# First stage of a hybrid layer: decays and score ahead of the numerator's norm, and six smaller moves

## The chip, the cores and the metric

One Trainium2 chip, all eight cores, one program. Each core computes half the output rows of one of four sequences, with no traffic between cores. The metric is the device time in microseconds of the slowest core.

## The reference

```python
# one layer, x (4, 4096, 1024) f32
h = rmsnorm(x, norm_mix_pre)
q_m,k_m,v_m,i_m,f_m,o_m, q_f,k_f,v_f,f_f, g_a,g_b = split(h @ w_in)
# A: mLSTM, 4 heads, dqk 128, dv 256
log_i = 15*tanh((i_m+b)/15);  log_f = log_sigmoid(15*tanh((f_m+b)/15))
C_t = f_t C_{t-1} + i_t v_t k_t^T;  n_t = f_t n_{t-1} + i_t k_t
h_a = rmsnorm((C_t q_t) / max(|n_t.q_t|, 1), ml_head_norm) * sigmoid(o_m)
# B: forgetting attention, 8 heads of 128, F = cumsum(log_sigmoid(f_f + b))
h_b = softmax(q_t.k_s/sqrt(128) + F_t - F_s, s <= t) @ v_f
merged = sigmoid(g_a+ba) * (h_a @ w_branch_a) + sigmoid(g_b+bb) * (h_b @ w_branch_b)
x = x + rmsnorm(merged @ w_out, norm_mix_post)
# channel mixing: causal width-3 convolution between up-projection and gate
a, g = split(causal_dwconv(rmsnorm(x, norm_ffn_pre) @ w_up, conv_w, conv_b))
x = x + rmsnorm((gelu(g) * a) @ w_down, norm_ffn_post)
```

## The kernel before, in words

Each core has 32 blocks of 128 tokens. Blocks 0 to 14 are a prefix, of which only the mLSTM state and the attention's keys and values are needed; 15 to 31 are its own (15 for two edge tokens only). A small framework records operations per engine in program order and inserts semaphore waits from what each reads and writes. So **the order in which the Python code calls `pg.add` is the order of every engine's queue**, and each engine works its queue strictly in order. Stages follow each other: mixing stage (to about 445 us), attention, merge, output projection, channel mixing.

**Mixing stage.** `A_load`, `A_sq` (square on ACT, then `rms_rstd`: a DVE step and a power on POOL), `A_sc` (DVE) and `A_T` (eight transposes on TensorE, one DVE copy) bring a block in. `W_load` and `W_cast` bring the weights in, with casts on ACT, DVE or POOL. `A_G` multiplies a block by the 16 gate columns; after each eight blocks `gates_slot` turns them into log gates (DVE add, ACT tanh, DVE times 15, ACT exponential, ACT ln, DVE sign) and `gates_slot2`, a step later, into cumulative gates (two small f32 matmuls, ACT and DVE steps). Four such slots cover the 32 blocks.

The main loop runs over the blocks in the order `MSEQ` (0 to 14, 16 to 23, 15, 24 to 31), `c` the block now, `cn` the next. A prefix block costs K and V projections and `upd`, the state update (matmuls at L825 and L827, four DVE steps `stt` at L525). A block of the own part (sixteen with an output of 128 rows, and 15) goes through these steps, in queue order: `num_mm(c)` (numerator and normaliser on TensorE L776 to L787; squares on ACT L791; small DVE steps; power on POOL L803), `I_mm(cn)` (decay matmuls into bank `SB0`, score matmuls into `SB1`, exponential of the decays on ACT, mask on POOL L748), `k_trans(cn)`, `num_fin(c)` (norm and output gate: four DVE steps), `V_proj(cn, 0)`, `I_fin(cn)` (two DVE steps: scaled queries `qs`, and `ST` = score times masked decays, which frees `SB1`), `A_T` of an input block, `V_proj(cn, 1)`, `upd(c)` (whose first half writes `SB1`), `ctb` (state scaled on ACT, L533), `O_proj(cn)` (tanh on ACT; POOL adds one, L719). Every fourth block is *fresh*: `QK_proj` computes queries and keys of the next four blocks. mm groups all carry line 385, small DVE helpers lines 522 (`tt`), 525 (`stt`) and 529 (`sts`), ACT's helper line 533. At two blocks POOL also issues weight DMAs (`load_qk`, `load_v`, L349), and at eleven a conversion DMA (L849).

**Attention.** `proj_pieces(h)` gives projections of head h in pieces (q, k: L1067; v: L385), whose banks DVE empties (`evac`, L1044); head 0's run alone, the others' between the steps of the head before. A step is `qk(n+1)`, an exponential on ACT (L1188), `pv(n-2)` (L1208). Two edge queries per head go through `e_qk` (24 matmuls of two columns, L1124, a DVE step, exponential L1131) and `e_pv`.

**Merge and output.** The merge runs for each of eight column chunks over five token tiles (edge, then four of 512), each with four mm groups that read `haT`, `hbT` and `xnT_own`. The output projection takes two mm groups a block, then a square on ACT, `rms_rstd`, a DVE product (L1445), two additions and a second square; `E1_scale` (DVE, L1397) prepares blocks for the channel mixing.

## Time and profile before

| | |
|---|---|
| median of 3 runs | 1790.73 us (1788.42 to 1964.29) |
| profiled execution | 1789.04 us, span 1787.5 us on core 7 |
| spans of the cores | 1782.1 to 1787.5 us, mean granted clock 0.980 to 0.983 |
| TensorE (PE) busy | 1658.5 us (93%) |
| DVE / ACT / POOL busy | 843.6 (47%) / 905.0 (51%) / 520.1 us (29%) |
| chain that ended last | PE 81%, ACT 6%, DVE 5%, issue 5%, POOL 2% |

Times are microseconds from the start of the span. "Idle before" is the time that the engine stood still ahead of an instruction, with the one that released it. Matmuls are pipelined, so neighbouring ones overlap. Granted clock 1.00 is the 2.4 GHz level, 0.50 the 1.2 GHz level.

### The profile page before, as it was taken

To read this page: it belongs to the slowest core of one execution; us is meant where nothing else is said; L and a number is where in the kernel's file an instruction comes from. 1 tells how busy PE (TensorE), PEld (TensorE's weight loads), DVE (VectorE), ACT (ScalarE), POOL (GpSimd) and SP (SyncE) were. 2 spreads that over 40 slices of the span, in tenths; PEclk is the share of its full clock that TensorE was granted. 3 is DMA by queue.
4 is the path that set the end of the run, shared out by engine and by line. 5 is a ranking of instruction groups with operands and counts; after the bars stand their busy time and mean duration, and the time that the engine had idled before them with its cause. 6 is when DMAs were issued, how large, how long until landed. Compare 5 with 4: busy or idle time off the path is not lost.

```text
span 1787.5 us, 36755 instructions; the slowest of 8 cores (1782.1 to 1787.5 us)
## 1 busy us (share of the span) xinstructions
PE 1658.5 (93%) x12584; PEld 924.1 (52%) x12584; DVE 843.6 (47%) x1599; ACT 905.0 (51%) x1711; POOL 520.1 (29%) x614
## 2 busy tenths in 40 slices
PE   4788897898999999999999799999899999999997
PEld 2444454444666767766767444444345444444443
DVE  4673545344343343343343122322577478386681
ACT  3554555445176676666767612222565256263461
POOL 2130443424021121110111123322563344343342
PEclk9899999999999999999999999999999999999999
DMA  9451335530831230230213232121756343343421
GB/s 296 140 171 47 74 75 89 79 64 19 124 46 15 39 45 14 37 40 19 34 28 70 68 83 95 49 94 50 213 202 215 72 165 125 112 162 85 155 95 48
DMA packets 102085, 163.26 MB, mean 91 GB/s; under 512 B 72848, under 2 KB 75152, under 8 KB 92688
## 3 DMA queue, kind: packets, MB, share of 16 engines
q1 hardware_dynamic: 78432, 134.50, 24.5%
q0 software_dynamic: 23040, 25.69, 10.3%
q8 instruction: 106, 1.74, 0.4%
q10 hardware_dynamic: 432, 0.72, 0.1%
q14 instruction: 75, 0.61, 0.1%
HBM read 160.63 MB, written 30.15 MB: 107 GB/s over the span
## 4 chain that ended last, share of the span: by engine, by line
PE 81%; ACT 6%; DVE 5%; issue 5%; POOL 2%; DMA 1%; ACTq 0%; DVEq 0%; POOLq 0%; SPq 0%
PE psum L385 50%; PE psum L1067 10%; PE psum L1616 9%; PE psum L1208 6%; PE psum L1539 5%; DVE arena L525 2%; ACT arena L1188 2%; ACT arena L533 1%; DVE arena L522 1%; ACT arena L791 1%; PE psum L825 1%; DMA arena<-x 1%; POOL arena L803 1%; DVE arena L491 1%; PE psum L510 1%
## 5 line engine op out<-in xcount | busy, mean ns | idle before, releaser
L385 PE MATMUL psum<-arena 128*128 128x512 bf16 (+4 forms) x6932 | 1153.2, 312 | 51.9 <-ACT arena L1188 16.2
L385 PEld LDWEIGHTS psum<-arena 128*128 128x128 bf16 (+1 forms) x6932 | 556.2, 99 | 505.2 <-issue 93.2
L1188 ACT ACTIVATE arena<-psum,arena 128x512 bf16<-128x512 f32 (+1 forms) x576 | 371.9, 653 | 176.2 <-PE psum L385 163.2
L1572 DVE SCALAR_TENSOR_TENSOR arena<-psum,arena 128x511 f32<-128x511 f32 x352 | 255.0, 747 | 47.5 <-POOL arena L1561 18.5
L1044 DVE CAST arena<-psum 128x512 bf16<-128x512 f32 (+2 forms) x176 | 113.4, 648 | 250.5 <-PE psum L1067 138.8
L1067 PE MATMUL psum<-arena 128*128 128x512 bf16 (+2 forms) x896 | 222.4, 354 | 4.6 <-DVE arena L1044 3.6
L1208 PE MATMUL psum<-arena 128*128 128x129 bf16 x2112 | 215.4, 221 | 1.4 <-POOL arena L1193 1.2
L1208 PEld LDWEIGHTS psum<-arena 128*128 128x128 bf16 x2112 | 156.4, 98 | 71.1 <-issue 4.2
L1193 POOL TENSOR_TENSOR arena<-arena 128x128 bf16<-128x128 bf16 x128 | 59.4, 471 | 349.4 <-ACT arena L1188 347.8
L1616 PE MATMUL psum<-arena 128*128 128x512 bf16 x704 | 153.1, 379 | 0.4
L1555 ACT ACTIVATE arena<-psum,arena 128x512 f32<-128x512 f32 x176 | 136.2, 781 | 21.4 <-PE psum L385 19.1
L1587 POOL TENSOR_TENSOR arena<-arena 128x512 bf16<-128x512 f32 x88 | 112.1, 1273 | 112.9 <-ACT arena L1584 102.5
L355 POOL TENSOR_TENSOR arena<-arena 128x1 f32<-128x1 f32 x82 | 51.2, 628 | 224.2 <-DVE arena L352 222.6
L1067 PEld LDWEIGHTS psum<-arena 128*128 128x128 bf16 x896 | 82.1, 98 | 58.7 <-issue 9.4
L1616 PEld LDWEIGHTS psum<-arena 128*128 128x128 bf16 x704 | 68.5, 98 | 84.1 <-issue 1.8
L525 DVE SCALAR_TENSOR_TENSOR arena<-arena,psum 128x256 f32<-128x256 f32 (+1 forms) x188 | 81.3, 477 | 61.7 <-PE psum L1208 43.5
L1335 ACT ACTIVATE arena<-psum,arena 128x512 f32<-128x512 f32 (+1 forms) x40 | 24.1, 603 | 141.9 <-PE psum L385 141.9
L533 ACT ACTIVATE arena<-psum 128x512 f32<-128x512 f32 (+3 forms) x110 | 61.0, 561 | 68.1 <-PE psum L385 67.8
L1347 POOL TENSOR_TENSOR arena<-arena 128x512 bf16<-128x512 f32 (+1 forms) x40 | 44.2, 1106 | 163.0 <-DVE arena L1344 162.8
L533 ACT ACTIVATE arena<-psum,arena 128x256 bf16<-128x256 f32 x128 | 53.5, 473 | 71.6 <-PE psum L385 71.5
L1341 DVE TENSOR_TENSOR arena<-psum,arena 128x512 f32<-128x512 f32 (+1 forms) x40 | 23.4, 586 | 139.4 <-ACT arena L1335 128.8
L719 POOL TENSOR_SCALAR arena<-arena 128x512 f32<-128x512 f32 x34 | 52.3, 1543 | 114.4 <-ACT arena L533 114.4
(117 smaller groups left out, 1315.3 us busy)
## 6 DMA issues: line engine op xcount, KB each, us to landing
arena<-wup_scr SPq DMA_DIRECT2D x44, 1024.0 KB, 4.9
arena<-x SPq DMA_DIRECT2D x33, 512.0 KB, 7.2
arena<-w_merge SPq DMA_DIRECT2D x32, 512.0 KB, 5.6
arena<-w_mem SPq DMA_DIRECT2D x12, 1024.0 KB, 12.0
wup_scr<-w_up POOLq DMA_DIRECT2D x11, 1024.0 KB, 10.9
arena<-x SPq DMA_DIRECT2D x8, 1024.0 KB, 6.7
out<-arena SPq DMA_DIRECT2D x16, 512.0 KB, 2.9
arena<-w_fox POOLq DMA_DIRECT2D x24, 256.0 KB, 4.6
```

The lines of the kernel that those rows point to most:

```text
L385: ins = e.matmul(out_ap, lhsT=l, rhs=r, start=(i == 0), stop=(i == n - 1))
L525: pg.add("dve", lambda e: e.scalar_tensor_tensor(out=o, in0=a, scalar=sc_, in1=b_, op0=op0, op1=op1), reads=rd, writes=wr)
L533: pg.add("act", lambda e: e.activation(out=o, in_=a, func=func, scale=scale, bias=bias), reads=rd, writes=wr)
L1044: pg.add("dve", lambda e: e.tensor_copy(out=out_ap, in_=in_ap), reads=rd, writes=wr)
L1067: ins = e.matmul(bank(bk)[:, 0:w_], lhsT=Wqk.ap[:, kc, which * P:(which + 1) * P], rhs=tv[:, kc, :], start=(kc == 0), stop=(kc == KC - 1))
L1188: pg.add("act", lambda e: e.activation(out=pt.ap[:, c0:512], in_=bank(lgb)[:, 0:512 - c0], func=AF.Exp, scale=float(P) ** -0.5, bias=bias_ ...
L1208: ins = e.matmul(bank(ACC[tl % 2][i // 2])[:, (i % 2) * 129:(i % 2) * 129 + 129], lhsT=pt.ap[:, i * P:(i + 1) * P], rhs=vx[s_].ap[:, j, :] ...
L1539: e.matmul(bank(bk)[:, 0:w_], lhsT=l, rhs=r, start=(kc == 0), stop=(kc == KC - 1))
L1555: pg.add("act", lambda e, ups=ups, yb=yb, cidx=cidx, ag=ag, w_=w_: e.activation(out=yb.ap[:, ag, 0:w_], in_=ups[:, 0:w_], func=AF.Identity ...
L1572: pg.add("dve", lambda e, ups=ups, yb=yb, cidx=cidx, sh=sh, jw=jw, ag=ag, w_=w_: e.scalar_tensor_tensor(out=yb.ap[:, ag, sh:w_], in0=ups[: ...
L1587: pg.add("pool", lambda e, yb=yb, gl=gl, fi=fi, w_=w_: e.tensor_tensor(out=actb.ap[:, fi, 0:w_], in0=gl.ap[:, 0:w_], in1=yb.ap[:, 0, 0:w_] ...
L1616: ins = e.matmul(bank(bs[hh]), lhsT=actb.ap[:, fc, bl * P:(bl + 1) * P], rhs=Wdn(fc)[:, hh * 512:(hh + 1) * 512], start=(fc == 0), stop=(f ...
```

## The change

1. Own tiles: `num_mm` is cut. Its matmuls stay, its other steps become `num_post`, called after `I_mm` and `k_trans` of the next tile (ahead of them where the next tile is fresh). `I_fin(cn)` moves from after `V_proj(cn, 0)` to ahead of `num_fin(c)`. The addition of one to the output gate moves from POOL (two halves) to DVE (one instruction in `num_post`).
2. `gates_slot` is cut in three: addition and tanh; times 15 and exponential after `V_proj(cn, 0)`; ln and sign after `V_proj(cn, 1)`. `gates_slot2` uses bank `SB1` while the next tile is a prefix one. `QK_proj(16)` goes ahead of the update of block 14.
3. Prologue: load order x0, w0, w1, x1; K projection of block b-1 in place of b-2; casts 2 and 3 ahead of the last gate matmul, 4 and 5 inside the gate chain.
4. Attention: for head 0 every second emptying of a bank is on ACT; the edge exponential is issued three steps after `e_qk`; the query projection of the edge block has 2 columns in place of 128.
5. The merge reads `hbT` with a dependency per head and token tile. `E1_scale` of a block comes one step later.

```diff
--- before.py
+++ after.py
@@ gates_slot
             acti(cap8.ap, gates.ap[:, :, 0:8], AF.Tanh, [gates], [cap8], scale=1.0 / 15.0)
+
+        def gates_slot_b():
             sts(gates.ap[:, :, 0:8], cap8.ap, 15.0, [cap8], [gates])
             acti(e1.ap, gates.ap[:, :, 4:16], AF.Exp, [gates], [e1], scale=-1.0)
+
+        def gates_slot_c():
             acti(spl.ap, e1.ap, AF.Ln, [e1], [spl], bias=1.0)
             sts(LF.ap, spl.ap, -1.0, [spl], [LF])
-        def gates_slot2(s_):
+        def gates_slot2(s_, gb):
...
@@ O_proj
-                pg.add("pool", lambda e: e.tensor_scalar(out=gw.ap[:, sl], in0=gw.ap[:, sl], scalar1=1.0, scalar2=None,
-                                                         op0=ALU.add), reads=[(gw.u, ho)], writes=[(gw.u, ho)])
@@ num_mm
+
+            def num_post(c):
+                par = MPOS[c] % 2
+                hb_, gw = hablk[par], Gw[par]
                 for h in range(4):
                     pg.add("act", lambda e, h=h: e.activation(
...
+                pg.add("dve", lambda e: e.tensor_scalar(out=gw.ap, in0=gw.ap, scalar1=1.0, scalar2=None, op0=ALU.add),
+                       reads=[(gw.u, 0), (gw.u, 1)], writes=[(gw.u, 0), (gw.u, 1)])
                 tt(sc.ap[:, par, 1, :], sc.ap[:, par, 5, :], sc.ap[:, par, 5, :], ALU.mult, [un], [un])
...
@@ prologue
-            for it in ("x0", "x1", "w0", "w1", "x2", "x3", "x4", "x5", "x6", "x7", "w2", "w3", "w4", "w5"):
+            for it in ("x0", "w0", "w1", "x1", "x2", "x3", "x4", "x5", "x6", "x7", "w2", "w3", "w4", "w5"):
...
-            for b in range(2, 8):
+            for b in range(1, 8):
                 if b < 7:
                     A_sq(b + 1)
                 A_sc(b)
-                K_proj(b - 2)
+                if b < 7:
+                    K_proj(b - 1)
                 A_T(b)
                 A_G(b - 1)
+            W_cast(2)
+            W_cast(3)
             A_G(7)
             gates_slot(0)
+            W_cast(4)
+            gates_slot_b()
+            gates_slot_c()
+            W_cast(5)
...
@@ main loop
+                fresh = own(cn) and NPRE + tile_of[cn][0] == cn
                 if own(c):
                     gs = G_all()
                     num_mm(c)
+                    if fresh or not own(cn):
+                        num_post(c)
                 elif own(cn):
+                    QK_proj(cn)
                     upd(c, 0)
                     upd(c, 1)
...
                 if own(cn):
-                    QK_proj(cn)
+                    if own(c):
+                        QK_proj(cn)
                     I_mm(cn)
                     k_trans(cn)
+                    if own(c) and not fresh:
+                        num_post(c)
+                    I_fin(cn)
                 if own(c):
                     num_fin(c, 0)
                     num_fin(c, 1)
                 if cn is not None and (own(cn) or cn > 5):
                     V_proj(cn, 0)
+                if gs is not None:
+                    gates_slot_b()
                 if late is not None:
-                    gates_slot2(late)
+                    gates_slot2(late, TB if own(cn) else SB1)
                 gs2 = gs
-                if own(cn):
-                    I_fin(cn)
                 if tails:
                     A_T(tails[0])
                 if cn is not None:
                     V_proj(cn, 1)
+                if gs is not None:
+                    gates_slot_c()
...
@@ attention
+                if both and evn[0] % 2:
+                    pg.add("act", lambda e: e.activation(out=out_ap, in_=in_ap, func=AF.Copy), reads=rd, writes=wr)
+                    return
...
-                for (t0, w_) in KT_TILES[4:]:
-                    chain(t0, w_, 0, 8 if w_ == P else 2)
+                chain(TPRE + P - 2, 2, 0, 8)
+                for (t0, w_) in KT_TILES[5:]:
+                    chain(t0, w_, 0, 2)
...
+            def e_exp(h):
                 pg.add("act", lambda e: e.activation(out=pE.ap, in_=lgE.ap, func=AF.Exp), reads=[lgE], writes=[pE])
...
                     if nl == 5:
                         e_qk(hl)
+                    if nl == 8:
+                        e_exp(hl)
@@ merge and output
-                            rd = [src]
+                            rd = [(src.u, (h, eb0 if eb0 else "E")) for h in range(8)]
...
-                en_ = n - 4 if 4 <= n <= 8 else -1
+                en_ = n - 5 if 5 <= n <= 9 else -1
```

## Rows read from the trace of the kernel before

**Rows 1.** Windows of TensorE: length, busy time (instructions), mean granted clock, DMA share, GB/s

```profile
190.00:445.00 255.00, 217.61 (x1512) 0.95 0.38 68
...
410.11:415.79 5.68, 5.68 (x25) 0.70 0.05 19
...
423.42:427.41 3.99, 3.99 (x24) 1.00 0.06 24
...
153.00:159.00 6.00, 5.55 (x20) 0.51 0.01 3
```

**Rows 2.** Waits of TensorE, 190 to 450 us: total, times, longest

```profile
PE psum L825 <- DVE arena L522: 30.9, 13, 5.5
...
PE psum L1067 <- DVE arena L1044: 3.2, 1, 3.2
```

**Rows 3.** Timeline of one own tile (start, duration, engine, line, operation, idle before)

```profile
403.55 0.83 PE L385 MATMUL psum<-arena 128*128 128x128 bf16 x12
...
404.93 0.39 ACT L791 ACTIVATE arena<-psum 128x256 bf16<-128x256 f32 x1
...
405.31 0.59 ACT L533 ACTIVATE arena<-psum 128x512 f32<-128x512 f32 x1
...
405.59 0.16 DVE L525 SCALAR_TENSOR_TENSOR arena<-arena 128x4 f32<-128x4 f32 x1 [1.09 <-ACT arena L791]
...
405.90 1.04 POOL L803 TENSOR_TENSOR arena<-arena 128x4 f32<-128x4 f32 x1 [0.92 <-DVE arena L525]
...
407.11 1.66 DVE L525 SCALAR_TENSOR_TENSOR arena<-psum,arena 128x256 bf16<-128x256 f32 x4 [0.99 <-POOL arena L803]
...
409.28 0.69 DVE L522 TENSOR_TENSOR arena<-psum,arena 128x512 bf16<-128x512 f32 x1
...
410.11 0.27 PE L825 MATMUL psum<-arena 128*128 128x256 bf16 x1 [2.06 <-DVE arena L522]
...
411.21 0.91 ACT L533 ACTIVATE arena<-arena 128x256 bf16<-128x256 f32 x2 [2.21 <-DVE arena L525]
```

**Rows 4.** DVE groups by shape, 115 to 117 us: busy, mean ns

```profile
L529 DVE TENSOR_SCALAR arena<-arena 128x1024 f32<-128x1024 f32 x2 | 1.5, 751 | 0.0
```

**Rows 5.** Waits of TensorE, 95 to 190 us

```profile
PE psum L385 <- ACT arena L533: 9.0, 3, 5.4
...
PE psum L510 <- ACT arena L533: 1.8, 2, 0.9
```

**Rows 6.** Timeline around the second gate slot

```profile
95.65 1.28 ACT L533 ACT_TABLE_LOAD   x1 [4.74 <-DVE arena L522]
...
99.50 1.56 ACT L533 ACTIVATE arena<-psum,arena 128x256 bf16<-128x256 f32 x4
...
100.47 3.57 PE L385 MATMUL psum<-arena 128*128 128x512 bf16 x8 [5.42 <-ACT arena L533]
```

**Rows 7.** Waits of TensorE, 0 to 95 us

```profile
PE psum L385 <- DVE arena L529: 3.6, 1, 3.6
...
PE psum L385 <- ACT arena L470: 2.9, 1, 2.9
```

**Rows 8.** Timeline in the attention, at an edge exponential

```profile
557.09 0.24 ACT L1131 ACTIVATE arena<-arena 128x48 bf16<-128x48 f32 x1 [2.33 <-DVE arena L525]
...
558.07 0.38 PE L385 MATMUL psum<-arena 128*128 128x512 bf16 x1 [1.14 <-ACT arena L1188]
```

**Rows 9.** Timeline of TensorE at the start of the merge

```profile
1016.52 230.17 PE L385 MATMUL psum<-arena 128*128 128x2 bf16 x1272 [4.29 <-DMA arena<-arena]
```

**Rows 10.** Waits of TensorE, 1015 to 1790 us

```profile
PE psum L385 <- DVE arena L1445: 4.7, 3, 1.6
```

**Rows 11.** Timeline in the prologue and the prefix: POOL powers, one DVE product

```profile
8.99 0.56 POOL L355 TENSOR_TENSOR arena<-arena 128x1 f32<-128x1 f32 x1 [5.71 <-DVE arena L352]
...
12.21 1.64 POOL L355 TENSOR_TENSOR arena<-arena 128x1 f32<-128x1 f32 x1 [2.66 <-DVE arena L352]
...
89.62 2.82 DVE L491 SCALAR_TENSOR_TENSOR arena<-arena 128x1024 bf16<-128x1024 f32 x1
```

32 lines of the change are left out of this document (12 added, 20 removed).

## The prediction

> **What bounds the kernel now.** I read the table of cores first: 1782.1 to 1787.5 us, both dies alike, so one explanation serves all. The page gives TensorE 93% busy, so the kernel is its matmul work plus what idles or slows it: 129 us of idle in a span of 1787.5. The question is how much of that the edits reach. The windows and the waits of TensorE place it. In the part with the sixteen mLSTM tiles that are emitted (190 to 445 us) TensorE is busy 217.6 of 255 us and its clock averages 0.95 of full [rows 1]; 30.9 us of the idle time are thirteen waits of the state update (L825) for one DVE line, L522 [rows 2]. The timeline of one such tile shows what is behind them [rows 3]. The last matmul of V is out at 408.05 (410.11 less the wait of 2.06). The update needs the bank of the score product, which is free only when DVE has written ST at 409.28 + 0.69. DVE got there last because its queue ran: variance (405.59), a wait of 0.99 for the power on POOL, four products of the numerator's norm (407.11, 1.66 us), the scaled queries, ST. On ACT the exponential of the decays (405.31) stood behind four squares. So a norm that nobody needs for 10 us is ahead of the one thing that TensorE waits for.
>
> **The clock is part of the price.** Half of the stalls are paid twice. After the wait that ends at 410.11 the mean granted clock was 0.70 to the next numerator, after the like wait that ends at 423.42 it was 1.00, and the same update and two output projections took 5.68 against 3.99 us [rows 1]: 1.7 us more, part of it at the 1.2 GHz level. Over the 255 us a mean of 0.95 is 0.05 x 255 = 12.8 us, some 12 of it under work. Of six waits of 2.05 to 2.07 us five were followed by such a drop, as were both long ones (4.87 and 5.47); of the five of 1.53 to 1.92 us none. Stage total within reach: 30.9 + 12.1 = 43.0 us.
>
> **Part 1, the emitted tiles (12 tiles with no query projection in between).** New order on ACT: exponential of the decays, squares; on DVE: k copy, norm's small steps, scaled queries, ST, then the norm's products. Times from the numerator's first matmul (T, 402.47 in the timeline). Decay and score matmuls start at T + 1.08 (403.55), the decays are out by about T + 1.7; exponential 0.59, to T + 2.35; four squares at 0.57 each, to T + 4.65; variance, which starts 0.66 after the last square does (404.93, 405.59) and is done by about T + 5.0; scaled queries and ST, which together took 1.2 after the norm's end (407.11 + 1.66 = 408.77 to 409.97), so with 0.1 to start to T + 6.3; update at T + 6.45. V is out at T + 5.58, so about 0.9 us of wait stays, where 2.06 was. The period of such a tile is then 6.45 + 0.54 (update) + 3.45 (two output projections, 3.99 less 0.54) = 10.45 us, against 13.3 and 11.65 before. What is late next: the squares on ACT and the variance behind them, since DVE's queue still puts the variance ahead of ST.
> Five of the twelve tiles (16 to 18, 20, 21) carry an input tile too. There the ring runs over DVE and ACT: variance 0.35, queries and ST 1.3, norm 1.65, copy of the transposed input 0.65, first state product 0.5, four state scalings 1.7 (411.21 is their start), tanh 0.6, square of the input 1.1, tanh 0.6, exponential 0.6, squares 2.25: 11.3 us, against 10.3 of TensorE's work; I take 11.6, of which 1.3 is wait, because the power on POOL now runs beside DVE (rival 2). With 7 x 0.9, 5 x 1.3 and 1.5 more for the tile with the gate chain, 14.3 us of wait remain, all below 1.9 us, so I count no drop of the clock: 43.0 - 14.3 = **28.7 us**. The wait of 5.47 at tile 24 goes too: POOL had two additions of one (L719) ahead of three weight DMAs, one conversion DMA and the power, and the change takes the additions from POOL. They go to DVE, 17 of [128 x 1024] f32 at about 0.75 us: the nearest row is a DVE multiplication by a scalar of that size, 751 ns [rows 4]. It is hidden in the 2 us in which DVE would wait for the squares (T + 2.85 to T + 4.9); with no cover it would cost 0.75 per tile, 12.8 in all. Queued behind the queries' multiplication, which now waits for the variance, are norm, copy and state products; each of them was later before. Bounds for this part: 33 (waits of 0.6) and 8 (each wait 1 us longer through the port, and the clock dropped after five of them, 12 + 5 x 1.7 = 20.5 less).
>
> **Part 2, ahead of tile 16.** Gate chain, slots 1 and 2: TensorE waits 9.0 us in three pieces for ACT, the longest 5.4 [rows 5]. In the timeline [rows 6] ACT loads a table at 95.65, does the tanh, waits for DVE, loads again, and only at 99.50 drains the banks of V that the projection at 100.47 needs. With the parts spread, V's first bank is drained right after the tanh (97.2), the next projection starts at about 98.1 in place of 100.47: 2.35 us, twice. The second wait then falls from 3.40 to 1.05 us, and the 5.9 us at 0.51 of the clock behind it [rows 1] come back: 2.9. The cumulative gates go to another bank than the transposes: the two waits of 0.9 (1.8 in [rows 5]) go. Sum 4.7 + 2.9 + 1.8 = **9.3**; from below 4.6, if the clock drops anyway and the table loads, two a slot as before, meet other work. Queued behind DVE's multiplication in part c, which waits for ln, are the state update and the next input scaling, needed a projection later: nothing. QK_proj(16) ahead of the last prefix update covers a wait of 0.84: **0.8**.
> Prologue: the first weight cast no longer stands behind x2, so the first K projection starts about 5 us sooner, but each K projection now needs the transpose just before it and its copy (0.69 + 0.3 exposed, less a gate matmul of 0.35), and one cast on DVE (1.2) and one on ACT (1.9) now stand ahead of and inside the gate chain. That chain ends later by about 2 us, and the waits of 3.6 and 2.9 us [rows 7] for it and for the cast shrink by as much. **0**, with bounds of 2 either way.
>
> **Part 3, attention.** At tile 31's end the second projection bank waits for DVE behind the norm (3.2 us, [rows 2]); with every second copy on ACT the third projection can start at once and the fourth is late by about 1.7: **1.5** (0 to 3). In each head the exponential of the two edge queries stands in ACT's queue while it waits 2.33 us for DVE, and TensorE then waits 1.14 us [rows 8]; eight heads, and three steps of delay cover the DVE step of 0.21. The exponential itself (0.24) still takes 0.1 of ACT's small lead: 8 x 1.05 = **8.4** (4 to 9). The query projection of 2 instead of 128 columns: 8 matmuls a head from 0.055 to 0.03 us, as the 24 of two columns beside it took 0.74: **1.4** (0 to 1.6).
>
> **Part 4, merge and output.** The merge's first tile needs only the edge columns, which have been there for long; it waits 4.29 us for the last transposed tile [rows 9]. Per-tile waits move that to the fifth tile, some 20 us on: **4.2**. In the output projection three waits, 4.7 us [rows 10], come from DVE standing in E1_scale for POOL's power of the same row block; one step later it is there. DVE then has 3.6 us of work against 3.46 of TensorE in five steps: **4.0** (2 to 4.7).
>
> Sum: 28.7 + 9.3 + 0.8 + 0 + 1.5 + 8.4 + 1.4 + 4.2 + 4.0 = 58.3 us. The profiled execution took 1789.0 (span 1787.5): 1789.0 - 58.3 = **1731 us**; the median of the runs shown, 1790.7, is 1.7 above it, which I leave out.
>
> **Rival 1, the forecast**: 1731.
> **Rival 2, the waits move to the port between DVE and POOL.** A DVE product on two SBUF tensors took 2.82 us beside a POOL cast; a power of one column on POOL took 1.64 when a DVE product was running, and 0.56 alone [rows 11]. In the new order the mask on POOL runs beside the addition of one, and the power beside the scaled queries. If each collision puts 1 us into the chain, waits are near 2 us again and the clock keeps dropping: part 1 gives 8 to 12 in place of 28.7, and the time is about 1731 + 18 = 1749 (up to 1752, and 1760 with low values in the other parts). Against it: whichever began first was not lengthened, and the queries start 0.2 us ahead of the power. The Trainium skill (GPSIMD Engine Reference, Specifications) says that POOL's SBUF interfaces are shared with VectorE where a DVE instruction runs in a two-port mode or has two SBUF inputs; by that both new neighbours collide in every tile, which is this rival's time. By that, rows 11 agree for the case of two inputs.
> **Rival 3, the norm was not what held the tile**: if the ring over DVE and ACT stays as long as it was, part 1 gives nothing and the other parts their 29.6, of which some 26 hold: 1763. Against it: without norm and power ahead of the state products the ring is shorter by arithmetic.
> **Rival 4, slower.** The clock stays at the lower level through the stage, because TensorE would still stop about once in each tile. At 0.5 a stage with about 205 us of full-speed matmul work takes 410 instead of 255: 1789 - 30 + 155 = 1914. It turns the sign when such stretches cost 58 us more than I count, and passes 2% slower at 94. Against it: from 222.5 to 278 us, four waits of up to 1.9 us went by at a clock of 1.00. The Trainium skill (TensorE: Matmul & The Clock Gate, "A second HAM failure mode: psum-queue depth-cycling") tells of a kernel whose short stops between matmul groups keep the clock switching; by it this rival would hold. The waits below 2 us speak against that here.
> **Rival 5, better**: ring and clock recover fully and waits of 0.3 us remain: 1731 - 15 = 1716.
>
> **Chances.** Forecast 0.60, rival 5 0.06, rival 2 0.22 (four fifths of it below 1754.9), rival 3 0.10, rival 4 0.02. Within 2% is about what a measurement can tell from no change: 1754.9 to 1826.5. Faster 0.60 + 0.06 + 0.18 = 0.84, same 0.04 + 0.10 = 0.14, slower 0.02. The range takes in the forecast, rival 5 and most of rival 2, and the lower bounds of parts 2 and 3: 1713 to 1760.
>
> **What the profile after would show.** Right: L825's waits for L522 at 10 to 16 us in place of 30.9, none above 2; clock of the tile part at 0.99; tiles without input at 10.5 us; merge without its wait; the edge exponential without a wait of TensorE; tile 16 reached about 10 us sooner. Wrong: DVE products at 1.3 us or more inside the tiles (rival 2), tiles at 11.8 with the waits on another line (rival 3), or a clock below 0.9 (rival 4). The forecast fails most easily at the remaining wait per tile: 1 us of it is 12 us of the sum, and more with the clock.

## The result, and the profile after

The kernel after takes 1735.0 to 1739.4 us, the kernel before 1788.4 and 1790.7: a ratio of 0.9704 (95% interval 0.9669 to 0.9739), 53 us less, where 58 were forecast (1731, range 1713 to 1760). Executions in which the cores of a die ran at a lower clock than the others are left out of this and of all ratios below. The kernel after was run once more, on the chip of h2, h3 and h4 below: 0.9703 (0.9684 to 0.9721).

To see where the time came from, the program is cut at five places, each the first start of a line's instructions in the view by line, read on every core and averaged over the eight: the numerator (L776 before and after), the first query projection of the attention (L1067, after L1088), the first copy out of the merge (L1344, after L1370), the first scaling in the output projection (L1445, after L1471), the start of channel mixing (L1539, after L1565).

| part (us, mean of 8 cores) | before | after | after, second run | change | forecast |
|---|---|---|---|---|---|
| start to first numerator | 186.0 | 179.5 | 179.1 | -6.5, -6.9 | -10.1 |
| own tiles | 254.7 | 230.5 | 229.9 | -24.2, -24.8 | -28.7 |
| projections, attention, wait ahead of the merge | 575.5 | 560.4 | 559.2 | -15.1, -16.3 | -15.5 |
| merge | 236.4 | 234.0 | 234.4 | -2.4, -2.0 | 0 |
| output projection | 55.7 | 50.7 | 50.7 | -5.0 | -4.0 |
| channel mixing | 476.2 | 476.5 | 476.2 | 0 | 0 |
| whole span | 1784.5 | 1731.6 | 1729.5 | -52.9, -55.0 | -58.3 |

The rows of after are from core 7, as those of before are. First the windows of TensorE (length, busy, mean granted clock, DMA share, GB/s), which answer to [rows 1]:

```profile
182.00:412.00 230.00, 210.23 (x1532) 0.98 0.42 75
390.02:400.38 10.36, 9.58 (x74) 1.00 0.08 27
298.00:303.00 5.00, 4.79 (x26) 0.66 0.00 0
278.00:286.00 8.00, 6.82 (x72) 0.57 0.11 32
```

Then the waits of TensorE from 182 to 412 us, the own tiles, which answer to [rows 2]:

```profile
PE psum L831 <- DVE arena L522: 7.6, 12, 0.8
PE psum L776 <- ACT arena L533: 5.4, 6, 2.5
PE psum L385 <- ACT arena L533: 4.5, 7, 1.1
PE psum L385 <- DVE arena L522: 2.2, 5, 0.5
```

The update's waits fell from 30.9 to 7.6 us, and an ordinary tile (second window) takes 10.36 us at full clock. But two other lines have grown, and around 280 and 300 us the clock is near half. The timeline of an ordinary tile is that of [rows 3] in the new order:

```profile
391.10 0.83 PE L385 MATMUL psum<-arena 128*128 128x128 bf16 x12
...
391.86 0.60 ACT L533 ACTIVATE arena<-psum 128x512 f32<-128x512 f32 x1 [0.73 <-PE psum L385]
...
392.35 0.38 ACT L795 ACTIVATE arena<-psum 128x256 bf16<-128x256 f32 x1
...
392.72 1.75 POOL L750 TENSOR_TENSOR arena<-arena 128x512 f32<-128x512 f32 x1 [6.57 <-DVE arena L735]
...
393.27 1.22 DVE L522 TENSOR_TENSOR arena<-arena 128x4 f32<-128x4 f32 x1
...
394.88 0.16 DVE L525 SCALAR_TENSOR_TENSOR arena<-arena 128x4 f32<-128x4 f32 x1
394.96 0.68 DVE L522 TENSOR_TENSOR arena<-arena 128x512 bf16<-128x512 bf16 x1
...
395.56 0.68 DVE L522 TENSOR_TENSOR arena<-psum,arena 128x512 bf16<-128x512 f32 x1
...
396.39 0.27 PE L831 MATMUL psum<-arena 128*128 128x256 bf16 x1 [0.78 <-DVE arena L522]
...
396.68 1.66 DVE L525 SCALAR_TENSOR_TENSOR arena<-psum,arena 128x256 bf16<-128x256 f32 x4 [0.44 <-POOL arena L809]
```

The exponential (391.86) is now ahead of the squares, and the norm's products (396.68) are behind the update. The chain that remains is squares, variance (394.88), queries, ST. Note the product of four columns at 393.27: it takes 1.22 us where it starts during GpSimd's mask (392.72 + 1.75). Here it is hidden, since DVE waits for the squares anyway.

Ahead of the own tiles (95 to 182 us, which answers to [rows 5]), and for the later parts (412 to 1260 us, [rows 8] and [rows 10]), the waits of TensorE are:

```profile
PE psum L385 <- ACT arena L533: 4.7, 3, 3.0
PE psum L385 <- DVE arena L522: 1.8, 1, 1.8
```

```profile
PE psum L385 <- ACT arena L1212: 4.8, 19, 0.5
PE psum L1088 <- DVE arena L1065: 4.7, 8, 2.0
...
PE psum L385 <- DVE arena L1471: 0.6, 1, 0.6
```

One wait of the first fence is new: 1.8 us for DVE, at the decay products of tile 16. One that it leaves out has grown: the transposes wait 1.5 us for DVE's scaling of an input block (L491), where it was 0.7.

Tile by tile on core 7 (from numerator to numerator in the timelines), the own tiles gave:

| tiles | before | after | forecast |
|---|---|---|---|
| 24, 25, 26, 28, 29, 30 (no input tile) | 82.1 | 62.5 | 62.7 |
| 16, 17, 18, 20, 21 (input tile too) | 62.7 | 56.3 | 58.0 |
| 22 (input tile and gate chain) | 15.9 | 13.0 | |
| 23 and 15 | 43.9 | 49.2 | |
| 19 and 27 (eight projections of the next tiles) | 48.0 | 48.0 | |

So the eleven tiles whose period was worked out came, in both groups, as forecast or better, and the whole shortfall of the part stands in two tiles that became 5.3 us longer.

### The profile page after: what moved, and what is told of

Same layout as the page of the kernel before. It is cut to its first block, busy times and chain, and to the rows that moved or that the text cites. A ratio compares the mean times of both kernels' runs of the same rounds, so it can differ in the third digit from the quotient of the medians.

```text
span 1737.8 us, 36721 instructions; the slowest of 8 cores (1725.9 to 1737.8 us)
## 1 busy us (share of the span) xinstructions
PE 1646.0 (95%) x12584; PEld 922.4 (53%) x12584; DVE 859.5 (49%) x1605; ACT 905.7 (52%) x1722; POOL 482.5 (28%) x580
## 3 DMA queue, kind: packets, MB, share of 16 engines
q0 software_dynamic: 23040, 25.69, 11.6%
q8 instruction: 106, 1.74, 0.4%
## 4 chain that ended last, share of the span: by engine, by line
PE 83%; DVE 5%; ACT 5%; issue 4%; DMA 2%; POOL 1%; POOLq 0%; SPq 0%; DVEq 0%; ACTq 0%
PE psum L385 51%; PE psum L1088 10%; PE psum L1642 8%; PE psum L1232 6%; PE psum L1565 5%; DVE arena L525 2%; ACT arena L1212 2%; DVE arena L522 1%; ACT arena L533 1%; DMA ha_scr<-arena 1%; DMA arena<-x 1%; PE psum L831 1%; PE psum L510 1%; ACT arena L483 1%; ACT arena L795 0%
## 5 line engine op out<-in xcount | busy, mean ns | idle before, releaser
L1065 DVE CAST arena<-psum 128x512 bf16<-128x512 f32 (+3 forms) x165 | 104.8, 643 | 252.0 <-PE psum L1088 137.8
L1088 PE MATMUL psum<-arena 128*128 128x512 bf16 (+3 forms) x896 | 221.1, 351 | 5.4 <-DVE arena L1065 4.7
L1642 PE MATMUL psum<-arena 128*128 128x512 bf16 x704 | 153.1, 379 | 0.6 <-POOL arena L1613 0.4
L355 POOL TENSOR_TENSOR arena<-arena 128x1 f32<-128x1 f32 x82 | 56.5, 695 | 241.6 <-DVE arena L352 233.5
L1088 PEld LDWEIGHTS psum<-arena 128*128 128x128 bf16 x896 | 80.6, 98 | 60.0 <-issue 11.3
L1565 PE MATMUL psum<-arena 128*128 128x512 bf16 x352 | 85.0, 376 | 0.0
## 6 DMA issues: line engine op xcount, KB each, us to landing
arena<-w_mem SPq DMA_DIRECT2D x12, 1024.0 KB, 11.6
```

The lines of the kernel that those rows point to most:

```text
L1065: pg.add("dve", lambda e: e.tensor_copy(out=out_ap, in_=in_ap), reads=rd, writes=wr)
L1088: ins = e.matmul(bank(bk)[:, 0:w_], lhsT=Wqk.ap[:, kc, which * P:(which + 1) * P], rhs=tv[:, kc, :], start=(kc == 0), stop=(kc == KC - 1))
L1565: e.matmul(bank(bk)[:, 0:w_], lhsT=l, rhs=r, start=(kc == 0), stop=(kc == KC - 1))
L1642: ins = e.matmul(bank(bs[hh]), lhsT=actb.ap[:, fc, bl * P:(bl + 1) * P], rhs=Wdn(fc)[:, hh * 512:(hh + 1) * 512], start=(fc == 0), stop=(f ...
```

## The experiments

Eighteen runs: parts of the change alone (e1, e2), the kernel after with parts undone, with work added (g2, g3) or with mends joined (g1 and h2, which are one kernel, and i2), and the kernel after again (h1). Own tiles and first numerator are means over the eight cores, as in the table above; timelines and tiles are from core 7 unless another is named.

**What held the own tiles: order or GpSimd (e1, e2, e3).** e1 is the kernel before with the norm moved behind decays, score product and transposed keys, and ST directly behind it:

```
-            def num_mm(c): ... squares, norm, power
+            def num_mm(c): ...            # numerator alone
+            def num_post(c): ... squares, norm, power
...
                     I_mm(cn)
                     k_trans(cn)
+                    if own(c) and not fresh:
+                        num_post(c)
+                    I_fin(cn)
```

> The kernel before with one part of the change: the numerator's norm (squares, small steps, power) is issued behind the decays, the score product and the transposed keys, and the scaled queries and ST directly behind it; the addition of one stays on GpSimd. Theory T (the norm in the queues of ACT and DVE was what held the state update): nearly all of the 23.7 us that the stage of the own tiles lost comes back here, 18 to 24 us in that stage, and tiles without an input tile have a period of 10.4 to 10.6 us. Rival G (the additions on GpSimd are a second holder: 2 x 1.54 us of them stand ahead of the mask and the power): periods of 11 us or more, and only 8 to 15 us in the stage. The total should fall by 18 to 25 us by T, 8 to 15 by G.

e2 is the kernel before with only `gw + 1` moved from GpSimd to VectorE, e3 the kernel after with it moved back:

```
-                pg.add("pool", lambda e: e.tensor_scalar(out=gw.ap[:, sl], ... scalar1=1.0 ...   # 2 x 512 columns
+                pg.add("dve", lambda e: e.tensor_scalar(out=gw.ap, in0=gw.ap, scalar1=1.0, ...   # in num_post
```

> The kernel before with only the addition of one moved from GpSimd (two of 512 columns a tile) to VectorE (one of 1024 columns, ahead of the norm's small steps). Theory T: it is no gain in the ordinary tiles, since in the old order DVE's queue is what is late: 0 to +0.75 us a tile for the worse (0 to 10 us slower), less some 3 us at tile 24, where the long wait of 5.47 falls to about 2. Rival G (GpSimd's queue holds the tile): 5 us or more faster in the stage.

> The kernel after with the additions of one back on GpSimd, all else as it is. If the port between DVE and GpSimd costs what the longer steps show (mask 1.59 in place of 1.26 us, power 1.25 in place of 1.05, four-column DVE steps of 1.2 to 1.5 us behind the addition), the own tiles get no slower, or faster by up to 0.5 us a tile (up to 6 us in the stage). If the relief of GpSimd is part of the gain (rival G), the stage is 5 us or more longer, above all at tile 24, where weight transfers are issued from GpSimd. Theory T says within 3 us in the ordinary tiles and 2 to 4 us longer at tile 24.

Measured: own tiles of 235.1 us in e1 (19.6 less than before; total 0.9879, 0.9863 to 0.9895), 248.3 in e2 (6.4 less; total 1781.7 us in two executions), 238.9 in e3 (8.4 more than after; total 0.9741, 0.9726 to 0.9756). TensorE's waits for ST, on core 7, by run, e1, e2, e3:

```profile
PE psum L827 <- DVE arena L522: 16.2, 12, 3.5
```

```profile
PE psum L825 <- DVE arena L522: 26.5, 14, 4.5
```

```profile
PE psum L831 <- DVE arena L522: 15.8, 12, 3.5
```

The order is the larger part, as theory T has it. The move of the additions is worth 6 to 8 us, where T put some 3 us at tile 24 and nothing elsewhere. On core 7 tile 24 gives 3.2 of the 5.2 us of e2 (its wait falls from 5.47 to 2.44) and 2.7 of the 7.7 us of e3; in e3 most of the rest stands in tiles 17, 18 and 21 (1.3, 1.3 and 0.9). The timeline of e3, in tile 17, shows how:

```profile
192.57 1.49 POOL L723 TENSOR_SCALAR arena<-arena 128x512 f32<-128x512 f32 x1
...
194.01 0.79 POOL L855 DMA_DIRECT2D wup_scr<-w_up  x1
194.22 1.92 DVE L525 SCALAR_TENSOR_TENSOR arena<-arena 128x4 f32<-128x4 f32 x1 [1.02 <-ACT arena L797]
194.82 1.28 POOL L752 TENSOR_TENSOR arena<-arena 128x512 f32<-128x512 f32 x1
...
196.06 0.68 DVE L522 TENSOR_TENSOR arena<-arena 128x512 bf16<-128x512 bf16 x1
...
196.66 0.68 DVE L522 TENSOR_TENSOR arena<-psum,arena 128x512 bf16<-128x512 f32 x1
```

An addition and the issue of a weight transfer stand ahead of the mask on GpSimd. The mask then runs at 194.82 to 196.10, over the variance, and this one, four columns wide, ends only at 196.14 in place of 0.16 us after its start. The queries behind it start at 196.06, and ST at 196.66. In the kernel after the mask starts 2.6 us earlier in the tile (2.7 us behind its first matmul, here 5.3) and hits a step that nobody waits for, and the wait of tile 17 is 0.66 in place of 1.91 us. The lengthening by GpSimd is rival 2's mechanism, but not the whole of these 1.25 us: ST also needs the mask, which ends only at 196.10, so without the lengthening it could have started some 0.5 us sooner (an estimate, 196.66 less 196.10). The rest is the late mask itself, that is GpSimd's queue. In the kernel before, the gain of e2 is for the most part waiting: TensorE's waits for ST fall from 30.9 to 26.5 us, its busy time by 0.7. Single tiles move by the clock, in both directions: tile 17 goes from 14.00 to 11.70 us when its wait falls from 2.05 to 1.46, tile 25 from 13.32 to 11.63 and tile 29 from 11.62 to 13.26 with waits as before.

**The gate chain (e4, f1, g4).** e4 is the kernel after with the chain in one piece everywhere and the gates' sums in the transposes' bank; f1 has only the chain of slot 3, which falls among the own tiles, in one piece; g4 only the bank as before.

```
                             gates_slot(found)
+                            if found == 3:          # f1; e4: always
+                                gates_slot_b()
+                                gates_slot_c()
```

> The kernel after with the gate chain in one piece again (tanh, exponential, logarithm in a row behind the gate matmuls) and the cumulative gates in the bank of the transposes. Ahead of the own tiles: 6 to 9 us more (the waits of 5.4 and 3.4 us and their half clock come back). In the own tiles two theories part. S (the parts of the chain, with one table load more and a half clock at the tile with the chain of slot 3 and the two behind it, are why the stage gave 23.7 and not 28.7 us): the tile with that chain and the next two together take 2 to 5 us less than the 62.2 us of the kernel after. C (these tiles are long for their input tiles and state steps, whatever the chain's form): 62 us or more. Total by S 3 to 6 us slower than after, by C 7 to 11.

> The kernel after with the gate chain of slot 3 alone in one piece (it runs beside the own tiles), while slots 1 and 2, ahead of the own tiles, stay in three parts. Theory S, from the run with the whole chain everywhere (its own tiles took 227.6 us against 230.5, but the first numerator came 7.0 us later): both gains together, own tiles 227.6 and first numerator at 179.5, total about 3 us faster than after and faster than every other kernel so far. Rival: it was the bank of the cumulative gates or the start offset of the stage against the input loads that gave those 2.9 us, and the total is within 1 us of after.

> The kernel after with the cumulative gates of slots 1 and 2 in the bank of the transposes again. The prediction's term: two waits of 0.89 us come back, the first numerator 1.8 us later. Rival: with the chain spread, ACT drains the bank sooner (the copy no longer stands behind the table loads), the waits stay at zero, and the first numerator comes within 0.5 us (beside a scatter of 2 us between cores, so the waits decide).

Measured: e4 186.5 to the first numerator (7.0 more than after) and 227.6 in the own tiles (2.9 less), total 0.9717 (0.9701 to 0.9732); f1 178.5 and 227.5, total 0.9702 (0.9666 to 0.9738), too wide to see 3 us, its profiled spans as a mean 4.3 and 2.2 us under those of the two runs of after; g4 181.4 (one execution), two waits of 0.9 us back. On core 7 tiles 22, 23 and 15 take 62.2 us in after, 58.8 in e4 and 58.9 in f1. Theory S holds as far as the form of slot 3's chain is what costs. The timeline of after, tiles 22 and 23, shows two table loads close together:

```profile
272.00 1.28 ACT L533 ACT_TABLE_LOAD   x1
272.12 1.89 PE L385 MATMUL psum<-arena 128*128 128x512 bf16 x8 [0.91 <-ACT arena L533]
...
275.43 0.27 PE L776 MATMUL psum<-arena 128*128 128x256 bf16 x1 [1.41 <-ACT arena L533]
...
276.10 1.28 ACT L533 ACT_TABLE_LOAD   x1
...
278.13 1.67 PE L385 MATMUL psum<-arena 128*128 128x128 bf16 x16 [1.13 <-ACT arena L533]
...
280.85 5.63 PE L385 MATMUL psum<-arena 128*128 128x128 bf16 x60 [1.05 <-ACT arena L533]
```

The logarithm is alone at the tile's end, so ACT loads a table for it and another for the tanh that follows. The first load (272.00) delays the logarithm and the scalings of the state, the second holds back the tanh that drains the output projections, the squares behind it and the copies of tile 15's queries and keys. The chain in one piece has two loads as well (in f1 at 258.56 and 268.68), so it is not a load more, as the expectation of e4 has it, but the place of the first: in f1 it falls at the start of tile 22 and shows in one wait of 2.22 us at the update, with a clock of 0.70 behind it, and tile 23 then takes 18.8 us in place of 22.6. In after three waits of 0.91, 1.41 and 1.13 us come within 7 us, the clock falls to 0.50 about 278 us and stays there to 285, and a fourth wait of 1.05 falls into that stretch. None of them is long.

**The state step at tile 15 (h3).** In the timeline of after the scalings of the state for tile 15's numerator (ACT, 296.96) come late:

```profile
294.62 2.25 DVE L525 SCALAR_TENSOR_TENSOR arena<-arena 128x256 f32<-128x256 f32 x4
...
296.96 1.71 ACT L533 ACTIVATE arena<-arena 128x256 bf16<-128x256 f32 x4 [3.50 <-DVE arena L522]
...
298.01 0.27 PE L776 MATMUL psum<-arena 128*128 128x256 bf16 x1 [2.52 <-ACT arena L533]
```

They start behind all four products and a sum, since the products are declared as writing the whole state. In the kernel before this wait was shorter:

```profile
309.84 0.27 PE L776 MATMUL psum<-arena 128*128 128x256 bf16 x1 [1.67 <-ACT arena L533]
```

h3 declares each product by its head:

```
-                            [St[1], St[0], aPR], [St[0]])
+                            [(St[1].u, h), (St[0].u, h), aPR], [(St[0].u, h)])
```

> The kernel after with the state step at tile 15 declared by head, and nothing else. Theory: the numerator of tile 15 waits 0.8 us in place of 2.52 and the clock does not fall behind it: the two tiles take 22.6 - 1.7 = 20.9 and 26.6 - 1.4 = 25.2 us, 3.1 us less together. Rival (the gain in the mended kernel came from the chain of slot 3 in one piece): under 1 us.

```profile
294.23 1.67 DVE L525 SCALAR_TENSOR_TENSOR arena<-arena 128x256 f32<-128x256 f32 x4
294.80 1.71 ACT L533 ACTIVATE arena<-arena 128x256 bf16<-128x256 f32 x4 [1.73 <-DVE arena L525]
...
295.86 0.27 PE L776 MATMUL psum<-arena 128*128 128x256 bf16 x1 [0.76 <-ACT arena L533]
```

On core 7 the tiles 23 and 15 take 20.72 and 25.19 us, 3.3 less than in after: 1.8 of wait and 1.5 of clock. The total is 0.9717 (0.9668 to 0.9765), too wide to see 3 us, and the mean of the own tiles, 229.1, is only 0.8 to 1.4 us under that of after. The timelines show why: tile 15 takes 25.2 us on all five cores read (0, 1, 2, 6, 7), but cores 0 and 6 have single waits of 3.4 to 4.3 us at tiles 22 and 26, and cores 0 and 1 come through the first tiles slowly at a clock of 0.81. At tile 26 of core 0 the squares stand 3.59 us for the DMA that stores an earlier tile's output from the buffer that they write; the kernel after has the like on core 3 (2.54 us, tile 22). No run here changes that wait.

In the kernel before tile 15 took 24.99 us. The change brought tile 23's update forward, the state's chain did not follow, and the wait grew to 2.52 us, behind which the clock fell (0.66 in the window above). e1, which changes the order alone, has the same wait of 2.52 and a tile 15 of 26.5 us.

**Ahead of tile 16 (e5, i1).** e5 undoes the order of loads, casts and first projections, and the place of tile 16's query projection; i1 only the latter:

```
                 elif own(cn):
-                    QK_proj(cn)
                     upd(c, 0)
...
-                    if own(c):
-                        QK_proj(cn)
+                    QK_proj(cn)
                     I_mm(cn)
```

> The kernel after with two early steps undone: loads, casts and K projections up to the first gate chain in their old order (the chain itself stays in parts that follow one another), and the query and key projections of tile 16 again behind the update of tile 14. By the trace of after the first update starts 0.7 us later than before (61.27 against 60.51) and the score product of tile 16 waits 1.77 us, with a lowered clock behind it, where 0.84 was. Theory P (both steps cost): the first update at about 60.5, the first numerator 1.5 to 4 us sooner than in after, total 1.5 to 4 us faster than after. Rival (the prediction's terms, 0 for the loads and casts and 0.8 of gain for tile 16): the first numerator 0 to 1.5 us later than in after.

> The kernel after with only the query and key projections of tile 16 again behind the update of tile 14. Theory Q (that step costs its wait of 1.77 us and the clock behind it, against 0.84 of wait saved, and hid in the run e5 behind the loss of the early steps): the first update as in after (58.5 to 59.0 us as a mean over the cores), the first numerator 2.5 to 3.5 us sooner, near 176.5. Rival P (the early steps are what costs): the first numerator within 0.8 us of after, 178.7 to 180.3.

| mean of 8 cores, us | before | after (two runs) | e5 | i1 |
|---|---|---|---|---|
| first update (first start of L831) | 60.0 | 58.5, 59.0 | 60.4 | 59.0 |
| first numerator | 186.0 | 179.5, 179.1 | 177.9 | 177.1 |

The totals are 0.9696 (0.9677 to 0.9715) in e5 and 0.967 (0.959 to 0.975) in i1, which can't tell 2 us. My theory P was half wrong: I had read the prologue on core 7 alone, whose first update was 60.4 in after; over all cores the new early order gains 1 to 1.5 us. Theory Q holds: tile 16's projection costs 2.0 to 2.4 us where it was put, by the two runs of after; five other kernels with the same first part (e3, e8, f1, g2, h4) reach the numerator at 178.5 to 179.0, by which it is 1.4 to 1.9. The timeline of after has this wait, and neither e5 nor i1 has it:

```profile
171.63 0.55 PE L385 MATMUL psum<-arena 128*128 128x128 bf16 x7 [1.77 <-DVE arena L522]
```

The decays of tile 16 are written to the bank in which the update of tile 14 leaves its sums of n. DVE reads them last, and the projection, 14 us of work that used to lie between, is now in front of both.

**The later parts (e6, h4, e8).** e6 undoes the later exponential, the merge's waits by tile and the later scaling; h4 only the merge's waits; e8 the copies on ACT and the two-column projection.

```
-                    if nl == 8:
-                        e_exp(hl)                                   # e6: again directly behind e_qk at nl == 5
-                            rd = [(src.u, (h, eb0 if eb0 else "E")) for h in range(8)]
+                            rd = [src]                              # e6, h4
-                en_ = n - 5 if 5 <= n <= 9 else -1
+                en_ = n - 4 if 4 <= n <= 8 else -1                  # e6
```

> The kernel after with three late steps undone, each in a part of the program of its own: the exponential of the edge queries issued right behind their score products, the merge's first matmul waiting for the whole transposed tensor, the output projection's scaling one step sooner. Theory: the part with the attention heads becomes 8 x 1.05 = 8.4 us longer, waits of 1.1 us back in each head, plus 4.3 us for the merge's wait in front of its first matmul; the merge behind it 2.4 us longer through the clock after that wait (a wait of 4.3 us with a clock of half speed behind it); the output projection 5.0 us longer. Total about 20 us slower than after. Rival: the wait for edge exponentials is only moved to another line, and the heads become less than 4 us longer; the merge's wait costs only itself, no clock, and the total is 10 to 14 us slower.

> The kernel after with the merge's matmuls waiting for the whole transposed tensor again, alone. Theory: one wait of 4.3 us ahead of the merge's first matmul, and 2.0 to 2.6 us more behind it at half the clock: total 6.3 to 6.9 us slower than after. Rival (the prediction's term): 4.2 us and no more.

> The kernel after with two steps undone: all copies of head 0's projections on VectorE, and the query projection of 128 columns where two are used. Theory (the prediction's terms): 1.5 + 1.4 = 2.9 us longer in the part of the projections and attention, the wait of 2.0 us for the second bank back at 3.2 us. Rival: GpSimd, VectorE and ScalarE are idle enough there that the copies are worth nothing and the narrower projection is worth nothing too, since loading weights sets its pace: under 1 us in all. A second way: the copies on ScalarE delay the start of the first attention head's exponentials, and undoing them is a gain of up to 1 us.

| part (us, mean of 8) | after (two runs) | e6 | h4 | e8 |
|---|---|---|---|---|
| projections to merge | 560.4, 559.2 | 575.0 | 563.9 | 561.7 |
| merge | 234.0, 234.4 | 236.1 | 236.1 | 235.3 |
| output projection | 50.7 | 54.9 | 50.7 | 50.7 |

The total of e6 is 0.9855 (0.9807 to 0.9903), that of e8 0.9716 (0.9702 to 0.9730). The edge exponential is the difference of e6 and h4: 11.1 us (9.9, if h4's 4.7 is taken from e6's 14.6 over after), forecast 8.4. On core 7 TensorE's waits for the heads' exponentials are 14.0 us in e6 and 4.8 in after:

```profile
PE psum L385 <- ACT arena L1212: 14.0, 28, 1.1
```

The merge's wait costs 3.5 to 4.7 us ahead of it and 1.7 to 2.1 in it, 5.6 and 6.4 by the two runs of after, where 4.2 were forecast; h4's total is 0.9738 (0.9722 to 0.9754), 6 to 7 us over the second run of after on the same chip. Its timeline and window show the wait and the clock behind it:

```profile
968.56 13.79 PE L385 MATMUL psum<-arena 128*128 128x2 bf16 x75 [4.21 <-DMA arena<-arena]
```

```profile
968.56:982.00 13.44, 13.44 (x75) 0.83 1.08 250
982.00:990.00 8.00, 8.00 (x39) 1.00 0.77 105
```

The output projection's term is 4.2 to 5.0 (forecast 4.0). e8 is worth 1.3 to 2.5 us (forecast 2.9), beside cores that differ by 6 us in that part; its wait for the second bank is 3.5 us, in after 2.0. But TensorE's waits for DVE's copies sum to 3.9 us in e8 (two waits) and 4.7 in after (eight), so what the copies on ACT give by themselves, and what the narrow projection, is not shown.

**A dose of waiting (g2, g3).** The kernel after with further squares in ACT's queue, ahead of the four real ones in each own tile; nothing is left out.

```
+                for h in [0] * extra:        # g2: 2, g3: 3
+                    pg.add("act", ... func=AF.Square, accum_out=sc.ap[:, par, 0, h:h + 1])
```

> The kernel after with two more squares of 256 columns (0.57 us each with their read of the sum) on ACT ahead of the numerator's four, in each own tile whose norm stands behind the decays; they write what the next square overwrites, so the output stays. A dose of 1.14 us: the wait ahead of the state update should rise from 0.79 to 1.93 us if squares, variance, queries and ST are one chain (tile period 11.5), by less if there is slack. By the theory that the clock falls only behind waits of about 2 us and more the clock stays at 1.00 in these tiles; by the rival (every longer wait costs clock) the period is over 12 us.

> As the run with two more squares, with three: a dose of 1.71 us, the wait at 2.5 us. If the price were linear the period of a tile without an input tile would be 12.07 us; if the clock falls behind such waits, as in the kernel before behind those of 2.05, it is 13.5 to 13.9 us, and the mean clock of the tile part falls from 0.97 to 0.92 or less.

Each ran once. The own tiles take 240.4 us in g2 and 258.8 in g3, after 230.5: two squares cost 10 us, the third alone 18. Windows of ordinary tiles on core 7, g2 (a wait of 1.74 us), then g3 (waits of 2.30, 2.39 and 2.30):

```profile
335.04:346.35 11.31, 9.57 (x73) 1.00 0.90 119
```

```profile
361.11:374.67 13.56, 11.26 (x73) 0.87 0.27 66
398.28:410.24 11.96, 9.57 (x74) 1.00 0.06 23
423.66:437.17 13.51, 11.21 (x73) 0.87 0.06 21
```

A wait of 1.74 us was paid once. One of 2.3 was paid with 1.6 us of slower matmuls in most tiles, though not in the one in the middle, at an even longer wait, nor in tiles 22 and 24 (2.30 and 2.36 us); and in tile 20 a wait of 1.91 was followed by a drop (0.88 over the tile). So the dose shows a steep price between 1.7 and 2.6 us, and no length that divides the two cases. The first two squares came to 0.95 and not 1.14 us, so 0.2 us of the chain was slack.

**Mended kernels (g1, h2, i2).** g1, run again as h2, joins f1, e5 and h3; i2 joins f1, i1 and h3, so it keeps the change's early order. h1 is the kernel after beside h2.

> The kernel after with three things: the gate chain of slot 3 in one piece (from the run f1), the early loads, casts and projections and tile 16's query projection in their old order (from the run e5), and the state step at tile 15 declared by head, so that the scaling of the state's first head for the next numerator (ACT) waits for that head's product alone and not for all four and the sum of n behind them. In the kernel after ACT starts these scalings at 296.96, 2.3 us after the first of the four products began, and the numerator waits 2.52 us, with a lowered clock behind it. Theory: the wait falls to 1 us or less and the clock stays up: the stretch of tiles 23 and 15 (275.43 to 324.63 in after, 49.2 us) takes 42 to 43.5 us, 3 us from the chain and 3 from the state step; the total is 6 to 8 us faster than after, 1728 to 1731. Rival: the numerator's second pair of heads only waits as much later, the clock drops as before, and the state step gives under 1 us.

> The kernel after, unchanged, for comparison on the same chip with the three beside it: 0.970 of the kernel before, first numerator at 179.5 as a mean over the cores, own tiles 230.5, output projection 50.7 us (up to 55 where the granted clock is below 1.00 without a wait).

> The mended kernel (slot 3's chain in one piece, old order of the early steps and of tile 16's projection, state step by head) beside the kernel after on one chip. By the stage times: own tiles 225.4 against 230.5, first numerator 0 to 1.5 us sooner, all else equal, so 5 to 6.5 us faster than the kernel after (ratio to before 0.966 to 0.967 against 0.970). Rival: what the tiles gain is given back by a lower clock in later parts that have no wait, and the two are within 2 us.

> The kernel after with the chain of slot 3 in one piece, the state step of tile 15 by head and tile 16's projections behind, and the early loads, casts and K projections as in after. By theory Q it is 1 to 2 us faster than the mended kernel of the run h2 (0.9679 of before there): ratio 0.966 to 0.968, first numerator near 176.5, own tiles 225.4. By rival P it is 0 to 1 us slower than that kernel.

| | ratio to before | first numerator | own tiles | span, mean of 8 |
|---|---|---|---|---|
| g1 | 0.9662 (0.9649 to 0.9675) | 178.2 | 225.4 | 1727.7 |
| h1 (after) | 0.9703 (0.9684 to 0.9721) | 179.1 | 229.9 | 1729.5 |
| h2 (as g1) | 0.9679 (0.9665 to 0.9694) | 178.1 | 225.5 | 1725.5 |
| i2 | 0.9639 (0.9596 to 0.9682) | 177.3 | 225.3 | 1724.7 |

i2 is the fastest kernel of the study: 1727.2 to 1732.3 us in six executions, median 1728.9, against 1733.7 to 1741.5 for the kernel after in its eight. The two were not run side by side, and the intervals of their ratios overlap or nearly touch. h2 is 3 to 4 us faster than h1 on one chip: its cores reach the attention 5.4 us sooner, 4.4 of it gained in the own tiles, and 1.8 us are given back in channel mixing (478.0 against 476.2), in i2 too (478.3). What does that was not looked into further.

## Why the prediction came close, and the step that failed

**The mechanism of part 1** was right: the norm was what held the update. The tile without input was forecast at 10.45 us and takes 10.36, its wait at 0.9 and is 0.78, the tile with input at 11.6 and takes 11.1 to 11.6, the cause being the one named, squares and variance. Rival 3 (the norm does not hold the tile) falls with e1. Rival 4 (the clock stays low) falls with the clock of 0.98 over the part. Rival 2's collisions exist, but hit a step with slack; against it I had said that whichever began first was not lengthened, and in e3 a variance that began 0.6 us ahead of the mask was. Rival 5 did not come: the waits that remain are those of the forecast.

**The step that failed in part 1** is the last of its sum, "With 7 x 0.9, 5 x 1.3 and 1.5 more for the tile with the gate chain, 14.3 us of wait remain, all below 1.9 us, so I count no drop of the clock". The windows from the first numerator to the attention's first projection, before and after, take it apart:

```profile
188.08:441.70 253.62, 217.13 (x1528) 0.95 0.38 68
181.76:411.80 230.04, 210.27 (x1530) 0.98 0.42 75
```

TensorE's idle time fell from 36.5 to 19.8 us, by 16.7, where 30.9 - 14.3 = 16.6 were forecast. Its busy time fell by 6.9 us, where 12.1 were counted for the clock. So the waits are right in their sum, and the clock is not: 5.2 us of it stayed, which is the whole shortfall of core 7 (23.6 in place of 28.7), and the stretches at 278 to 286 and 298 to 303 us hold some 4.5 of it (an estimate: busy time times what the clock lacks to 1.00). That the waits agree is luck. Those of the update came to 7.6 us in place of 14.3, and those of other lines grew from 5.5 to 12.1, above all since the gate chain of slot 3 and tile 15's state step were costed wrongly. I had weighed the spread chain ahead of tile 16, where it gains, and took it for a wait of 1.5 us in its own tile, where its loads fall on the scalings and copies that TensorE needs; by the sum's own terms that tile would have waited 0.9 + 1.5 = 2.4 us, which is not below 1.9. And I took tile 15's wait to stay at 1.67. Measured: 2.9 us for the chain (e4, f1) and, on core 7, 3.3 for the longer state wait with its clock (h3). Both together give back 6.4 us on core 7 in h2, and 4.4 to 5.1 us as a mean over the cores (h2 against h1, g1 against after), which covers the 4 to 4.5 us by which the part fell short.

**Unforeseen inside part 1**: I gave GpSimd's additions a part in tile 24 alone. e2 and e3 put them at 6 to 8 us, some 3 of it in that tile; with the norm alone (e1) the part gives 19.6 us. That the change came near 28.7 is in part luck: a step that was costed low was in it.

**Part 2.** The gate chain was forecast at 9.3 and measured at 7.0 to 7.4 (e4), the bank's share of 1.8 at 1.9 to 2.3 (g4). The waits themselves came as worked out: the first 3.00 us (5.42 less 2.35 is 3.07), the second 0.99 (forecast 1.05); what is smaller is the rest, the clock's share and what surfaces behind. Tile 16 was reached 6.5 to 6.9 us sooner, and not 10. "QK_proj(16) ahead of the last prefix update covers a wait of 0.84: 0.8" is the second step that failed, with the wrong sign: it costs 1.4 to 2.4 us (i1). I had listed what a moved step uncovers for the product and the queues, and not for the PSUM bank that two steps share. The prologue, forecast at 0 with 2 either way, gains 1 to 1.5.

**Parts 3 and 4** were low: 19.5 us in their sum against 22.5 to 23.3. Edge exponential 8.4 against 10 to 11, head 0 and narrow projection 2.9 against 1.3 to 2.5, merge 4.2 against 5.6 to 6.4, output projection 4.0 against 4.2 to 5.0. The merge is the term mis-sized: its wait was counted once, though part 1 of the same prediction counted such waits twice. The Trainium skill (TensorE: Matmul & The Clock Gate, "A second HAM failure mode: psum-queue depth-cycling") warns of short stops that keep the clock switching. The prediction set it aside for waits below 2 us; g2 agrees with that (1.74 us in an ordinary tile at a clock of 1.00), and the three waits of 0.9 to 1.4 us close together at tiles 22 and 23, with a clock of 0.50 behind them, speak for the page.

The forecast's distance, 1731 against 1735 to 1739, is then 4 to 4.5 us in part 1 and 3 to 4 ahead of it, less the 3 to 4 that the later parts gave beyond their terms. So the total came closer than its parts.

## What to carry to other kernels

A wait of TensorE has two prices, its length and the clock behind it. The second one is not proportional: 0.57 us more on ACT in each tile cost 5 us over the stage for each of the first two squares, and 18 for the third. Remove the waits that are just long enough to be followed by a drop, and after every reordering look for the ones that have just become so. When a step is moved, go through its banks as well as its queues: whose last reader does its write wait for? And splitting a chain moves its table loads, though their number stayed at two a slot here: look where each load falls, in every stage in which the chain is issued.

## What the runs showed of the hardware that was not expected

A VectorE instruction on four columns, 0.16 us by itself, ended with GpSimd's product of 512 columns beside it: 1.22 us at 393.27 in the kernel after, 1.92 at 194.22 in e3, where it had begun 0.6 us ahead of the product, while GpSimd issued a transfer.

The clock can be below full with no wait at all. In g1 core 3 went through the output projection without idling at 0.90 (0.81 from 1210 to 1220 us), and took 55.4 us; in h2 the same kernel had 1.00. The windows of the part, g1, then h2:

```profile
1197.20:1252.60 55.40, 55.40 (x234) 0.90 0.68 188
```

```profile
1195.20:1244.90 49.70, 49.08 (x230) 1.00 0.64 187
```

The two ran on different chips, but the chip alone does not decide it: in the same execution of g1 cores 0 and 1 took 50.8 us, and i1 and i2, on a chip of the same number, took 50.7 on every core. So a part's gain of 5 us, as that of the later scaling, can be hidden by the execution that is read. What lowers the clock there stays open.

Between 1.9 and 2.4 us the drop behind a wait isn't certain: 2.39 us went by at 1.00 in g3, where 2.30 did not in the tiles around it. At tile 22 f1 and i2 both waited 2.2 us; up to the next numerator the clock was then 0.70 in f1 (5.68 us) and 1.00 in i2 (3.99 us).
